# An expert layer on one core: gather and sum with whole f32 values instead of a high and a low part

## What is computed

```python
h = modulate(rms_norm(x, norm_ffn_g), sh2, sc2)
# router: sigmoid scores, 4 of 8 groups, 8 of 64 experts for a token, gates = their scores / sum * 2.5
out = (silu(h @ ws_gate) * (h @ ws_up)) @ ws_down              # shared expert, 1024 -> 256 -> 1024
for e in range(64):
    out = out + gates[:, e:e+1] * ((silu(h @ we_gate[e]) * (h @ we_up[e])) @ we_down[e])
x = x + g2 * out                                               # g2: the second gate, one row of 1024
return rms_norm(x, norm_final_g)
```

## Time and profile before

| | us |
|---|---|
| median of 3 runs (lowest to highest) | 695.98 (695.71 to 696.42) |
| the profiled execution, its span | 690.9, 689.1 |
| TensorE busy, its mean granted clock | 623.2 (90%), 0.972 of 2.4 GHz |
| VectorE, ScalarE, GpSimd busy | 256.1, 125.9, 44.4 |
| chain that ended last: TensorE, DMA, VectorE, ScalarE | 70%, 15%, 9%, 3% |
| HBM read over the span | 248.91 MB, 363 GB/s |

### The profile page before, as it was taken

How to read it: one execution, slowest core, us unless ns; L and a number is a source line. 1 busy time by engine, 2 the same in 40 slices (tenths; PEclk the granted TensorE clock), 3 DMA queues, 4 the chain that set the end, 5 groups by cost and what they waited for, 6 DMA issues and landing times.

```text
span 689.1 us, 11735 instructions
## 1 busy us (share of the span) xinstructions
PE 623.2 (90%) x4454; PEld 346.7 (50%) x4454; DVE 256.1 (37%) x704; ACT 125.9 (18%) x269; POOL 44.4 (6%) x225
## 2 busy tenths in 40 slices
PE   2599999999789999999899999979899999999792
PEld 0278877744445454454344445544445445544440
DVE  0129938869562233241323232331133132332115
ACT  2311312202510111211111111110111111111113
POOL 7000000000400000101000000010000001000000
PEclk9789999999998999999999999999999999999996
DMA  8996894565378999999999999999999999999951
GB/s 346 380 400 267 334 394 160 214 272 212 156 290 360 411 418 422 420 420 419 420 421 420 421 420 421 419 421 419 422 419 422 419 421 419 421 420 421 420 208 63
DMA packets 39868, 250.75 MB, mean 364 GB/s; under 512 B 4657, under 2 KB 6785, under 8 KB 11777
## 3 DMA queue, kind: packets, MB, share of 16 engines
q1 hardware_dynamic: 38256, 248.56, 88.1%
q10 hardware_dynamic: 1554, 1.41, 0.6%
HBM read 248.91 MB, written 1.05 MB: 363 GB/s over the span
## 4 chain that ended last, share of the span: by engine, by line
PE 70%; DMA 15%; DVE 9%; ACT 3%; issue 1%; SPq 1%; ACTq 0%; DVEq 0%
PE PS L1371 11%; PE PS L1581 10%; PE PS L1577 10%; DMA ring<-in_we_up_dram 9%; PE PS L1556 8%; PE PS L1618 5%; PE PS L1587 5%; PE PS L1613 4%; DMA ring<-in_w_in_dram 4%; PE PS L1640 3%; PE PS L1636 2%; PE PS L1623 2%; DVE MOD L885 2%; PE PS L1501 1%; PE PS L1596 1%
## 5 line engine op out<-in xcount | busy, mean ns | idle before, releaser
L1371 PE MATMUL PS<-hT,ring 128*128 128x256 f32 x384 | 86.8, 386 | 3.7 <-DMA ring<-in_w_in_dram 3.7
L1581 PE MATMUL PS<-ring,arena 128*64 128x256 f32 x736 | 88.4, 391 | 0.3 <-DMA ring<-in_we_up_dram 0.3
L1192 DVE SCALAR_TENSOR_TENSOR arena<-arena,gate,PS 128x128 f32<-128x128 f32 (+1 forms) x44 | 16.6, 378 | 175.8 <-ACT arena L809 175.8
L1371 PEld LDWEIGHTS PS<-hT,ring 128*128 128x128 f32 x384 | 73.8, 194 | 15.1 <-issue 5.2
L1203 DVE TENSOR_TENSOR YLO<-PS,YHI 128x512 fp32r<-128x512 f32 x54 | 37.2, 689 | 97.0 <-ACT YHI L820 97.0
L1556 PE MATMUL PS<-G,H2HI 128*128 128x256 f32 (+1 forms) x240 | 63.6, 300 | 10.4 <-ACT arena L800 7.0
L1577 PE MATMUL PS<-ring,arena 128*32 128x512 f32 x576 | 68.6, 628 | 3.8 <-DMA ring<-in_we_up_dram 3.8
L1581 PEld LDWEIGHTS PS<-ring,arena 128*64 128x64 f32 x736 | 50.3, 134 | 32.5 <-issue 4.0
L820 ACT CAST YHI<-PS 128x512 fp32r<-128x512 f32 x54 | 31.6, 586 | 161.4 <-PE PS L1618 79.2
L1556 PE MATMUL PS<-G,H2LO 128*128 128x256 f32 (+1 forms) x240 | 59.1, 281 | 0.0
L1556 PEld LDWEIGHTS PS<-G,H2HI 128*128 128x128 f32 x240 | 46.1, 192 | 22.7 <-issue 9.6
(11 more groups left out here) (265 smaller groups left out, 606.2 us busy)
## 6 DMA issues: line engine op xcount, KB each, us to landing
ring<-in_we_gate_dram SPq DMA_DIRECT2D x64, 1024.0 KB, 16.4
ring<-in_we_up_dram SPq DMA_DIRECT2D x64, 1024.0 KB, 19.2
ring<-in_we_down_dram SPq DMA_DIRECT2D x64, 1024.0 KB, 16.6
ring<-in_w_ada_dram SPq DMA_DIRECT2D x6, 3072.0 KB, 15.1
ring<-in_w_in_dram SPq DMA_DIRECT2D x3, 3072.0 KB, 15.9
ring<-in_w_ada_dram SPq DMA_DIRECT2D x3, 2048.0 KB, 7.1
ring<-in_w_out_dram SPq DMA_DIRECT2D x1, 3072.0 KB, 19.4
ring<-in_w_in_dram SPq DMA_DIRECT2D x1, 1568.0 KB, 26.8
```

Source lines behind the costliest of these rows:

```text
L1371: mm = pe.matmul(PS[:, 2 + q % QB, 0:TOK], w[:, k, (m % 6) * P:(m % 6) * P + P], hT[:, k, :], start=(k == 0), stop=(k == KD - 1))
L1581: m = pe.matmul(PS[64 * c:64 * c + 64, 6, 0:FE].rearrange("p (a n) -> p a n", a=2), xt[:, k, :], gu_cols(w[0], k, c), start=(k == 0), stop ...
```

## The change

- The split is gone: no H2HI, H2LO, YHI, YLO. gather reads H2P itself as stationary operand, with its step of 8 values, against an f32 G; add_up reads one f32 tensor Y and an f32 SCAT. Each pair of fp32r matmuls becomes one f32 matmul.
- VectorE multiplies each down product with its part of the second gate as it takes it out of bank 5 (gated), for NARROW and PAIR with gpair, which holds the two halves of the gate on the two row halves.
- In the first position VectorE forms gpair and adds g2 x shared expert to X (add_shared); the first sum then starts banks 0 to 3 anew (start at p == 0), and waits for that. At the end X + banks is one operation a tile.
- The scatter matrix waits for the sum two positions back. ScalarE's table for the square root is fetched after the last position. The shared expert's gate and up steps are regrouped between the router's steps. The branch for experts with too many tokens is changed alike; it is not taken with these inputs.

```diff
-        o[0] = 9256
-        H2P = part(2 * D).rearrange("p (t n) -> p t n", t=TT)
+        H2P = arena[:, 0:2 * D].rearrange("p (t n) -> p t n", t=TT)
+        GS = arena[:, 2 * D:4 * D].rearrange("p (t n) -> p t n", t=TT)
         SH = XTf[:, 0:TT * D].rearrange("p (t n) -> p t n", t=TT)
 
-        H2HI = nc.alloc_sbuf_tensor_at("H2HI", [P, TT, D], F32R, offset=h2_at)
-        H2LO = nc.alloc_sbuf_tensor_at("H2LO", [P, TT, D], F32R, offset=h2_at + 4 * TT * D)
-        YHI = nc.alloc_sbuf_tensor_at("YHI", [P, D], F32R, offset=y_at)
-        YLO = nc.alloc_sbuf_tensor_at("YLO", [P, D], F32R, offset=y_at + 4 * D)
-        G = nc.alloc_sbuf_tensor_at("G", [P, 2, TT, 256], F32R, offset=gffn_at)
+        Y = nc.alloc_sbuf_tensor_at("Y", [P, D], F32, offset=y_at)
+        gpair = nc.alloc_sbuf_tensor_at("gpair", [P, 512], F32, offset=y_at + 4 * D)
+        G = nc.alloc_sbuf_tensor_at("G", [P, 2, TT, 256], F32, offset=gffn_at)
         mod4_at = hT_at + 4 * (KD * TOK + 4 * D)
-        SCAT = nc.alloc_sbuf_tensor_at("SCAT", [P, 2, TOK], F32R, offset=mod4_at)
+        SCAT = nc.alloc_sbuf_tensor_at("SCAT", [P, 2, TOK], F32, offset=mod4_at)
...
-            for t in range(TT):
-                pool.wait_ge(h2_ready, t + 1)
-                pool.wait_ge(h2hi_ready, t + 1)
-                pool.tensor_tensor(H2LO[:, t, :].rearrange("p (k q) -> p k q", k=KD),
-                                   H2P[:, t, :].rearrange("p (q k) -> p k q", k=KD),
-                                   H2HI[:, t, :].rearrange("p (k q) -> p k q", k=KD).bitcast(F32),
-                                   ALU.subtract).then_inc(h2lo_ready, 1)
...
-            def high_part(t):
-                act.copy(H2HI[:, t, :].rearrange("p (k q) -> p k q", k=KD),
-                         H2P[:, t, :].rearrange("p (q k) -> p k q", k=KD)).then_inc(h2hi_ready, 1)
...
-            def y_high(p, h):
-
-                act.wait_ge(down_ps, parts_before(p) + h + 1)
-                act.copy(y_part(YHI, p, h), bank(5)).then_inc(yhi_ready, 1)
...
+            act.activation(small[:, 15:16], ident[:, 0:1], ACT.Sqrt)
...
             def scatter_matrix(p):
 
+                if p >= 2:
+                    dve.wait_ge(summed, p - 1)
                 dve.tensor_scalar(SCAT[:, p % 2, :], tokrow, tokf[:, p:p + 1], None,
                                   ALU.is_equal).then_inc(scat_ready, 1)
 
-            def y_low(p, h):
-
-                dve.wait_ge(yhi_ready, parts_before(p) + h + 1)
-                dve.tensor_tensor(y_part(YLO, p, h), bank(5), y_part(YHI, p, h).bitcast(F32),
-                                  ALU.subtract).then_inc(ylo_ready, 1)
+            def gated(p, h):
+
+                g = MOD[:, 5 * D + 512 * h:5 * D + 512 * h + 512] if halves(p) == 2 else gpair[:]
+                dve.wait_ge(down_ps, parts_before(p) + h + 1)
+                dve.tensor_tensor(y_part(Y, p, h), bank(5), g, ALU.mult).then_inc(y_ready, 1)
+
+            def add_shared():
+
+                dve.wait_ge(sy_ps, TT)
+                for t in range(TT):
+                    link(dve.tensor_tensor(GS[:, t, :].rearrange("p (a n) -> p a n", a=2), PS[:, 2 * t:2 * t + 2, :],
+                                           MOD[:, 5 * D:6 * D].rearrange("p (a n) -> p a n", a=2), ALU.mult))
+                    link(dve.tensor_tensor(X[:, t, :], X[:, t, :], GS[:, t, :], ALU.add), shared_added)
...
+                if p == 0:
+                    dve.wait_ge(modrow_ready, 8)
+                    dve.tensor_copy(gpair[0:64, :], MOD[0:64, 5 * D:5 * D + 512]).then_inc(gpair_ready, 1)
+                    dve.tensor_copy(gpair[64:128, :], MOD[64:128, 5 * D + 512:6 * D]).then_inc(gpair_ready, 1)
+                    dve.wait_ge(gpair_ready, 2)
+                    add_shared()
                 if place == 1 and i + 2 < len(UNITS):
                     gather_matrix(i + 2)
                     one_hots(i + 2)
                 for h in range(halves(p)):
-                    y_low(p, h)
+                    gated(p, h)
...
             dve.wait_ge(summed, NPOS)
-            dve.wait_ge(modrow_ready, 8)
             for t in range(TT):
-                link(dve.tensor_tensor(SH[:, t, :].rearrange("p (a n) -> p a n", a=2), PS[:, 2 * t:2 * t + 2, :],
-                                       MOD[:, 5 * D:6 * D].rearrange("p (a n) -> p a n", a=2), ALU.mult))
-                link(dve.tensor_tensor(X[:, t, :], X[:, t, :], SH[:, t, :], ALU.add), fin_ss)
+                link(dve.tensor_tensor(X[:, t, :].rearrange("p (a n) -> p a n", a=2), PS[:, 2 * t:2 * t + 2, :],
+                                       X[:, t, :].rearrange("p (a n) -> p a n", a=2), ALU.add), fin_ss)
...
-                        pe.wait_ge(h2hi_ready, TT)
-                        pe.wait_ge(h2lo_ready, TT)
+                        pe.wait_ge(h2_ready, TT)
                     last = max([m for m in range(n) if xt_bank(m) == xt_bank(n)], default=None)
                     if last is not None:
                         pe.wait_ge(xT_dve if last % 2 else xT_act, last // 2 + 1)
                     for half in range(2):
                         k = 2 * j + half
                         for t in range(TT):
-                            for part_no, h2 in enumerate((H2HI, H2LO)):
-                                m = pe.matmul(PS[:, xt_bank(n), 256 * half:256 * half + w], h2[:, t, k * P:(k + 1) * P],
-                                              G[:, i % 2, t, 0:w], start=(t == 0 and part_no == 0),
-                                              stop=(t == TT - 1 and part_no == 1))
+                            m = pe.matmul(PS[:, xt_bank(n), 256 * half:256 * half + w], H2P[:, t, k:D:KD],
+                                          G[:, i % 2, t, 0:w], start=(t == 0), stop=(t == TT - 1))
...
             def add_up(p):
 
-                pe.wait_ge(ylo_ready, parts_before(p + 1))
+                pe.wait_ge(y_ready, parts_before(p + 1))
                 pe.wait_ge(scat_ready, p + 1)
+                if p == 0:
+                    pe.wait_ge(shared_added, TT)
                 for t in range(TT):
-                    for y in (YHI, YLO):
-                        for c in range(2):
-                            if halves(p) == 2:
-                                m = pe.matmul(bank(2 * t + c), SCAT[:, p % 2, t * P:(t + 1) * P],
-                                              y_part(y, p, c), start=False, stop=True,
-                                              skip_group_check=True)
-                            else:
-                                m = pe.matmul(bank(2 * t + c), SCAT[64 * c:64 * c + 64, p % 2, t * P:(t + 1) * P],
-                                              y[64 * c:64 * c + 64, 0:512], start=False, stop=True,
-                                              skip_group_check=True)
+                    for c in range(2):
+                        if halves(p) == 2:
+                            m = pe.matmul(bank(2 * t + c), SCAT[:, p % 2, t * P:(t + 1) * P], y_part(Y, p, c),
+                                          start=(p == 0), stop=True, skip_group_check=True)
+                        else:
+                            m = pe.matmul(bank(2 * t + c), SCAT[64 * c:64 * c + 64, p % 2, t * P:(t + 1) * P],
+                                          Y[64 * c:64 * c + 64, 0:512], start=(p == 0), stop=True,
+                                          skip_group_check=True)
                 m.then_inc(summed, 1)
...
-            shared_gate_up(0, range(1, 3))
+            shared_gate_up(0, range(1, 2))
             logits(1)
-            shared_gate_up(0, range(3, KD))
+            shared_gate_up(0, range(2, KD))
...
-            shared_gate_up(1, range(1, 3))
+            shared_gate_up(1, range(1, 2))
             pe.wait_ge(sort_in, 1)
             pe.matmul(PS[0:1, 2, 0:NE - FIXED], idcol[0:NE, :], pick[0:NE, 0:NE - FIXED], start=True,
                       stop=True).then_inc(order_ps, 1)
-            shared_gate_up(1, range(3, KD))
+            shared_gate_up(1, range(2, KD))
```

More of the change, by code:

```diff
@@ L17 @@
 BF16 = mybir.dt.bfloat16
-F32R = mybir.dt.float32r
 U32 = mybir.dt.uint32
@@ L222, in build @@
         o[0] = 0
-        h2_at = arena_at
         o[0] = 2 * TT * D
@@ L329, in build @@
         h2_ready = sem("h2_ready")
-        h2hi_ready = sem("h2hi_ready")
-        h2lo_ready = sem("h2lo_ready")
         h2T_ps = sem("h2T_ps")
@@ L367, in build @@
         down_ps = sem("down_ps")
-        yhi_ready = sem("yhi_ready")
-        ylo_ready = sem("ylo_ready")
+        y_ready = sem("y_ready")
+        gpair_ready = sem("gpair_ready")
+        shared_added = sem("shared_added")
         scat_ready = sem("scat_ready")
@@ L385, in build @@
         more_down_ps = sem("more_down_ps")
-        more_yhi = sem("more_yhi")
-        more_ylo = sem("more_ylo")
+        more_y = sem("more_y")
         more_scat = sem("more_scat")
@@ L776, in _ @@
                          PS[:, 3 + 2 * t, :].rearrange("p (k n) -> p k n", k=4)).then_inc(h2T_ready, 1)
-                if t == 0:
```

(38 more changed lines are left out.)

## The result

The changed kernel takes 771.09 us (770.45 to 771.64) against 695.85 us before: 1.108 times the time, 95% interval 1.106 to 1.110. It is slower, as forecast, by 75.2 us where 54 were expected. The profiled execution had 771.03 us, span 769.1; that of before had 690.9, so between the two profiled executions there are 80.1 us.

A forecast was written before the change was run, and what follows sets the result against it. TensorE was taken as the tighter of two nearly full limits, with DMA. On the profiled 690.9 us, +76.5 - 12.9 - 5.3 - 3.6 = +54.7 gave 745.6; with the 5.1 offset 750.7, forecast 750, range 735 to 772.

The forecast's parts named there:

- rival 2: Gather: weight loads with a 32-byte step are slow, up to 24 us more, 774 us; chance 0.08.
- fp32r against f32 cadence: Gather, 256 columns: a high + low fp32r pair costs 0.236 us, the one f32 matmul replacing it 0.432.
- Strided weights cost nothing: Gather: reading H2P with a step of 8 values adds nothing; bound 0.05 us on each of 480 records, 24 us.
- 192 columns in proportion: Gather, 192 columns: an f32 record takes 0.162 us, in proportion to columns, adding 0.42 us a step.
- Sums: Adding up expert products: ten full-row positions add 16.2 us, 34 in 64-row halves add 25.2 us.
- Rival 1: Sums: f32 row halves don't overlap, 54 us more, 804 us; chance 0.05.
- What gives way: Expert stage: weight waits of 8.8 us, clock dips of 2.4 and the low part's wait of 1.7 go: -12.9 us.
- Start: Before the expert stage and in unit 0: without the split 4.2 us are gained there, -5.3 us in all.
- Offset: Whole kernel: the runs' median lies 5.1 us above the profiled execution, carried whole; 745 if a TensorE-bound kernel loses it.
- VectorE in position 0: First position: about 6.1 us of new VectorE work, covered by position 2's MIXED gate and up; at most some 3 us otherwise.
- End: After the last products: two multiplications leave the chain, -2.4 us; the last two products wait one copy less each, -1.2.

The follow-up runs named there:

- step 1: The changed kernel with H2P laid out so each block of 128 gather weights is contiguous (step of 1 value instead of 8): 746.82 us, 1.0728 of before.

## Why the prediction was right and where it was not

The direction and the main mechanism were right: two f32 passes for one fp32r pass, TensorE past the stream, no weight waits. The likeliest time, 750, was 21 us low, outside the 742 to 760 of the forecast itself; the range to 772 held 771.09 only through rival 2, and by 0.9 us, which is luck. Two errors make up the miss: the strided weights, put at nothing, cost 24.3 us, and the offset of 5.1 us was not there. 745.6 + 24.3 is 769.9, against 771.03 in the profiled execution.

- *fp32r against f32 cadence*: right. With contiguous weights the whole kernel takes 746.8, and its profiled execution (746.37) is 0.8 us from the 745.6 of the sum.
- *Strided weights cost nothing*: the step that failed. It rested on the transposes of the earlier trace rows, which carry the same operand and load it every 0.11 us. A matmul's load at that step takes 0.24. The bound given for it, 0.05 us on 480 records, 24 us, came from no row, and that it met the measured 24.3 is luck: with 256 columns the load costs 0.026 us on a record, with 192 some 0.08. Rival 2's chance of 0.08 was too small; it had a mechanism, and against it stood one row of another kind of instruction. The weight loads of those very transposes, 192 ns strided against 141, were in the trace of before and had not been read.
- *192 columns in proportion*: right where the weights are contiguous, 1.50 on the chain in step 1 against 1.07 before, +0.43 (0.42). In the changed kernel itself the step of weights took 2.15.
- *Sums*: right, 3.43 (3.46) full rows, 1.92 (1.87) half rows, the latter 34 x 0.05 = 1.7 us more. Rival 1 falls: f32 row halves run side by side.
- *What gives way*: right in the profile but for one wait. Weights are never waited for in the stage; L1591 still waits 0.9 us for the product, of the 1.7 that were to go.
- *Start*: the mask is used at 186.19 us on the chain instead of 189.55, 3.4 earlier (forecast 4.2), and the first PAIR takes 3.85 us instead of 5.60. At the median it is worth more, since the wait that lowers the clock is gone.
- *Offset*: I carried 5.1 us, and said that a kernel bound by TensorE might lose it. It was lost (771.03 profiled, 771.09 median), though it belonged to the start's clock and not to the stream.
- *VectorE in position 0*: right. Changed kernel, order of time:

```profile
225.27 0.41 DVE L1223 COPY gpair<-MOD 64x512 f32<-64x512 f32 x1
225.71 0.42 DVE L1224 COPY gpair<-MOD 64x512 f32<-64x512 f32 x1
226.17 1.23 DVE L1179 TENSOR_TENSOR arena<-PS,MOD 128x1024 f32<-128x1024 f32 x1
...
231.21 0.69 DVE L1173 TENSOR_TENSOR Y<-PS,gpair 128x512 f32<-128x512 f32 x1
234.71 0.48 DVE L1159 SCALAR_TENSOR_TENSOR arena<-arena,gate,PS 128x256 f32<-128x256 f32 x1 [2.81 <-ACT arena L788]
```

5.9 us of new work, done by 231.2, and VectorE then still waits 2.81 us for the MIXED gate and up that covers it.

- *End*: right. From the start of the last sum to the end of the span it is 769.1 - 757.56 = 11.5 us; before, with the sum at 675.77, 13.3. The sum itself is 0.8 longer, so 2.6 us were gained (2.4), and the last product's wait is 0.80 us instead of 1.41.

## What to carry to other kernels

Before a stationary operand is read with a step, look at whether neighbours still share 16 bytes. Up to 8 bytes it was free here to within 1.2 us; from 16 on a gather's load of 128 columns set a pace of 0.24 us, which two f32 passes of 256 columns nearly covered (0.216) and shorter ones did not. A price for an operand must come from the same kind of instruction, and the weight loads (PEld) must be read beside the matmuls: the transposes' pace hid a slower load. When one f32 matmul replaces a split pair, count passes and not instructions. And before paying them, look whether the cost of the split is its place on the chain: moved off it, the split kernel won 9 us.

## What was not expected of the hardware

- f32 and fp32r come to the same pace with strided weights, about 0.24 us a load (336 against 190 ns in the record), while transposes pay at most 0.01 us, with 193 against 141 ns in the record.
- Strided fp32r gather steps bring TensorE's clock down to 1.2 GHz with hardly any wait before them (nine times in the stage); f32 steps with the same loads don't.
- Without a step, fp32r of 192 columns is paced by something other than its columns: 0.110 us, near the 0.118 of 256.
- Behind the same wait of 2.97 us TensorE's clock falls to 1.2 GHz in one execution and stays at 2.4 in another, and the stretch behind it is 4.3 us longer, of a 696 us kernel.
- f32 matmuls on 64-row halves overlap as well as those on column halves do: 1.92 against 1.87 us for eight records of 512 columns.
